# The dt product with its 32 weight columns as the stationary side, in four column groups

## The chip, the cores and the metric

The kernel runs on one core of a Trainium2 chip. The metric is the device time of one execution in microseconds (us). Each kernel is run several times and the median is taken. A profile is one further execution, recorded by the hardware profiler. Its span runs from the first to the last instruction, and all times in the rows below are counted from the span's start.

## The reference: what is computed

One layer of a hybrid trunk for 128 prompt tokens and 256 latent tokens, 384 in all. The normalised and modulated input `h` is multiplied by one wide matrix `w_in`, and the result feeds a Mamba-2 scan, an RWKV-7 scan, an output projection and a mixture of experts. The change touches the 32 columns of `w_in` that give `dt`, two directions of 16 heads each:

```
u = (h @ w_in).astype(jnp.float32)
...
z, xbc, dt_raw = jnp.split(u, [M_INNER, M_INNER + M_XBC], axis=-1)
xbc = jax.nn.silu(centred_depthwise_conv(xbc, conv_w, conv_b))
...
dt = jax.nn.softplus(dt_raw.reshape(bsz, seqlen, 2, M_HEADS) + dt_bias)
a = -jnp.exp(a_log.astype(jnp.float32))
...
la = jnp.moveaxis((dt * a_head).reshape(bsz, nc, M_CHUNK, M_GROUPS, e), 2, -1)
cs = jnp.cumsum(la, axis=-1)
```

So `dt_raw` is a product of 384 tokens by 1024 inputs by 32 columns. `dt` and `la` are then needed for the decays of the Mamba scan.

## The kernel before, in words

All is in float32. `hT` holds the input transposed, 8 tiles of 128 inputs by 384 tokens. The weights of `w_in` and of the conditioning matrix `w_ada` come in blocks of 512 columns (2 MB) through four slots (three in `ring_a`, one in `um_a`). The queue of SyncE (SP) issues the load of a block as soon as the block that had the slot before is used up, in one fixed order.

TensorE (PE) goes through a program written out by hand, in this order around the change:

- `project` (line 1655) with the 12 column tiles of x, B and C. ScalarE (ACT) copies each out, VectorE (DVE) sums the five taps of the convolution, ACT applies silu, PE transposes, DVE copies the token-major form (`token_major`, line 2329), from banks 4 and 5 of PSUM in turn.
- The Z loop (line 1697): six products of eight steps each, 128 tokens by 512 columns, ACT applies silu (line 2039).
- Between these stand the pieces of the conditioning product. `ada_block` (line 1613) has `cond` with 32 columns as the stationary side, in four column groups: each group takes two of the eight input tiles and writes 32 partitions of one bank. ACT copies the bank to `adas` (line 2009). `ada_columns` (line 1623) adds the four groups and transposes, by four products of a 128x128 tile of `adas` with `sel32`, a selector of ones.
- The dt product (line 1711), behind the Z loop and the last conditioning pieces: for each of three token tiles eight steps with a 128x128 tile of `hT` as the stationary side and 32 columns of `wdt` as the moving side, 24 products into bank 7.
- `project` with the 27 column tiles of the RWKV half (counted t = 0 to 26), into banks 0 and 1 in turn. After t = 1 PE does `decay_sums` (lines 1719 to 1724), which waits for `la`, and `scores` (line 1733); after t = 2 `states_in` (line 1745), which waits for the loaded SSM states; t = 0 to 2 use one weight block, t = 3 to 6 the next.

Behind the dt product DVE adds the bias (line 2340), ACT loads the table of exp and ln (line 2046) and takes exponentials and the logarithm of the softplus (to line 2050), and DVE forms `dt` and `la` (to line 2352), which frees `decay_sums`. In ACT's program this stands behind the six silus of Z and the last two copies to `adas`. The semaphore `dt_ps` counts dt products, `act_m` ACT's steps on dt, `conv_tm` DVE's token-major copies.

The stages further on (the Mamba scan between the RWKV projections, the RWKV rounds, the output projection, the experts) are started by semaphores and slots that earlier work frees.

Of the kernel before, what the change touches and what calls it, by code (L numbers as in the profile page):

```python
# [10 lines left out]
ACT = mybir.ActivationFunctionType  # L11
# [6 lines left out]
P = 128  # L18
D = 1024
KT = D // P  # L20
NTILE = 3
T = NTILE * P
# [81 lines left out]
def program(nc, a, out):  # L104
    ctx = ExitStack()
    with ctx:
# [16 lines left out]
        sel32 = sb("sel32", [P, 32])  # L123
# [53 lines left out]
        st1 = xdw  # L177
        xd = scratch[:, 2048:3072].rearrange("p (b d c) -> p b d c", b=2, d=2)
        wkv_ld = st_tiles[0:64, :].rearrange("p (d c) -> p d c", d=2)
        hT_flat = hT[:, :, :].rearrange("p k t -> p (k t)")  # L180
# [1417 lines left out]
        def _(pe):  # L1598
# [90 lines left out]
            ada_columns(6)  # L1689

            for i in range(6):
                n, j = Z_N[i // 3], i % 3
# [7 lines left out]
                if j == 0:  # L1700
                    ada_columns(7 if i == 0 else 9)
                if j == 2:
                    ada_block(8 if i == 2 else 10)
                    ada_block(9 if i == 2 else 11)
                    ada_columns(8 if i == 2 else 10)
            ada_columns(11)

            pe.wait_ge(s_wdt, 16)
            for j in range(NTILE):
                for k in range(KT):  # L1710
                    mm = pe.matmul(ps[:, 7, 32 * j:32 * j + 32], hT[:, k, P * j:P * j + P], wdt[:, k, :],  # L1711
                                   start=(k == 0), stop=(k == KT - 1))
            mm.then_inc(dt_ps, 1)

# [261 lines left out]
        def _(act):  # L1976
# [57 lines left out]
            ada_copy(7)  # L2034
            conv_silu(XBC - 1)
            for i in range(6):
                act.wait_ge(proj, XBC + i + 1)
# [10 lines left out]
            act.activation(dtmp[:, :, :], dtmp[:, :, :], ACT.Exp).then_inc(act_m, 1)  # L2048
            act.wait_ge(act_m, 1)
            act.activation(dtl[:, :, :], dtmp[:, :, :], ACT.Ln, bias=1.0).then_inc(act_m, 1)  # L2050
# [210 lines left out]
        def _(dve):  # L2261
# [69 lines left out]
            for t in range(XBC):  # L2331
                taps(t)
                if t >= 3:
# [4 lines left out]

            dve.wait_ge(dt_ps, 1)
            chain.do(dve.tensor_tensor(dt[:, :, :], ps[:, 7, 0:96].rearrange("p (j h) -> p j h", j=NTILE),  # L2340
                                   drow[:, 0:32].unsqueeze(1).to_broadcast([P, NTILE, 32]), ALU.add))
            dve.scalar_tensor_tensor(dtmp[:, :, :], dt[:, :, :], -1.0, dt[:, :, :], ALU.mult,
                                     ALU.min).then_inc(dt_in, 1)
            dve.wait_ge(act_m, 2)
            chain.do(dve.tensor_scalar(la[:, :, :], dtmp[:, :, :], 1.0, None, ALU.add))
# [416 lines left out]
```

## Time and profile before

| what | value |
|---|---|
| median of 3 runs | 1160.0 us (1158.66 to 1160.59) |
| the profiled execution | 1157.79 us |
| its span | 1156.0 us, 34174 instructions |
| PE busy | 1092.4 us (94%) |
| PE weight loads busy | 692.8 us (60%) |
| DVE busy | 600.0 us (52%) |
| ACT busy | 338.8 us (29%) |
| GpSimd (POOL) busy | 127.8 us (11%) |
| chain that ended last | PE 91%, DVE 4%, issue 2%, ACT 1%, DMA 1% |
| moved by DMA | 206.80 MB, mean 179 GB/s |

The busy times of engines overlap, so they don't add up to the span. The chain that ended last follows the end of the kernel back through what each step waited for, and says which engine's work sets the time. A product in float32 shows as two records of PE and two weight loads (PEld), so 24 products are 48 records. PEclk is the granted clock of TensorE as a share of 2.4 GHz: 1.00 is 2.4 GHz and 0.50 is 1.2 GHz.

### The profile page before, as it was taken

The page shows a single profiled execution, that of the slowest core. Times are in us where ns is not written, and L with a number is a line of the kernel's source. Part 1 is how long each engine was busy: PE and PEld are TensorE (multiplying, and loading weights), DVE is VectorE, ACT ScalarE, POOL GpSimd, SP SyncE. Part 2 cuts the span into 40 slices and gives each one's busy share as a digit, 9 for nine tenths or more (in the row PEclk, how much of TensorE's full clock was granted, in tenths as well). Part 3 has the DMA queues.
Part 4 walks back from the last instruction along what each step waited for, and adds up shares of the span by engine and source line. Part 5 has one row for each costly group of instructions (what it writes and reads, how often), then busy time and mean ns, then how long its engine had stood idle before and what let it go on. Part 6 is the DMA issues. An engine that isn't in the chain of part 4 may idle for free.

```text
span 1156.0 us, 34174 instructions
## 1 busy us (share of the span) xinstructions
PE 1092.4 (94%) x15326; PEld 692.8 (60%) x15326; DVE 600.0 (52%) x1346; ACT 338.8 (29%) x792; POOL 127.8 (11%) x185
## 2 busy tenths in 40 slices
PE   5999999999999899999999999988999999999995
PEld 2755447666665576666666666665675555555543
DVE  1455002678857576575766667532673343334346
ACT  2222111444443454454535445322330000000002
POOL 6000000122003031130303113000000000000002
PEclk9999997999999899999999998989999999999999
DMA  9844643564220302021110201134388999999984
GB/s 329 318 146 155 238 171 118 164 164 146 92 73 1 92 29 77 20 74 40 48 59 28 77 20 40 31 112 115 113 356 338 416 417 416 417 415 416 367 345 164
DMA packets 82336, 206.80 MB, mean 179 GB/s; under 512 B 12852, under 2 KB 21399, under 8 KB 77591
## 3 DMA queue, kind: packets, MB, share of 16 engines
q1 hardware_dynamic: 74816, 186.71, 43.7%
q10 hardware_dynamic: 6519, 14.90, 3.6%
q0 software_dynamic: 864, 3.15, 0.8%
q8 instruction: 113, 1.85, 0.6%
q14 instruction: 24, 0.20, 0.1%
HBM read 193.15 MB, written 11.58 MB: 177 GB/s over the span
## 4 chain that ended last, share of the span: by engine, by line
PE 91%; DVE 4%; issue 2%; ACT 1%; DMA 1%; SPq 0%; DVEq 0%; PEldq 0%; ACTq 0%
PE ps L1655 17%; PE ps L1240 10%; PE ps L1229 8%; PE ps L560 6%; PE ps L623 5%; PE ps L1260 5%; PE ps L1697 4%; PE ps L1878 3%; PE ps L542 2%; PE ps L1613 2%; PE ps L1779 2%; PE ps L474 2%; PE ps L592 1%; PE ps L455 1%; PE ps L699 1%
## 5 line engine op out<-in xcount | busy, mean ns | idle before, releaser
L1655 PE MATMUL ps<-hT,ring_a 128*128 128x384 f32 x624 | 210.9, 493 | 0.9 <-DVE um_a L2382 0.9
L1655 PEld LDWEIGHTS ps<-hT,ring_a 128*128 128x128 f32 x624 | 117.4, 192 | 80.3 <-issue 5.3
L1229 PE MATMUL ps<-scratch,misc 128*128 128x128 f32 x864 | 99.6, 275 | 1.5 <-DVE misc L2714 1.5
L1229 PEld LDWEIGHTS ps<-scratch,misc 128*128 128x128 f32 x864 | 97.9, 192 | 3.1 <-issue 3.1
L1299 ACT ACTIVATE um_a<-ps 128x256 f32<-128x256 f32 x17 | 6.5, 383 | 271.9 <-PE ps L1240 271.9
L560 PEld LDWEIGHTS ps<-ring_a 32*32 32x32 f32 x6144 | 62.1, 105 | 36.9 <-issue 23.6
L2382 DVE SCALAR_TENSOR_TENSOR um_a<-ps,mum,um_a 128x252 f32<-128x252 f32 (+1 forms) x162 | 57.2, 409 | 51.1 <-ACT um_a L2060 50.1
L560 PE MATMUL ps<-ring_a 32*32 32x32 f32 x6144 | 70.6, 195 | 7.7 <-issue 7.7
L1240 PE MATMUL ps<-ring_a,um_a 128*64 128x512 f32 x288 | 63.4, 593 | 1.6 <-DVE um_a L1281 1.5
L1240 PE MATMUL ps<-misc,um_a 128*64 128x512 f32 x128 | 56.3, 592 | 1.4 <-DVE um_a L1281 1.4
L623 PE MATMUL ps<-ring_a,mixm 128*128 128x512 f32 x96 | 54.3, 647 | 0.0
L1293 DVE COPY um_a<-ps 128x256 f32<-128x256 f32 x17 | 7.2, 424 | 90.5 <-PE ps L1249 90.5
L1281 DVE COPY um_a<-ps 128x1024 f32<-128x1024 f32 x17 | 20.8, 1226 | 53.7 <-issue 49.8
L1240 PEld LDWEIGHTS ps<-ring_a,um_a 128*64 128x64 f32 x288 | 21.0, 137 | 42.1 <-issue 42.1
L2060 ACT ACTIVATE um_a<-ps,mum 128x384 f32<-128x384 f32 x27 | 15.7, 580 | 103.1 <-PE ps L1655 103.1
L1524 POOL TENSOR_SCALAR_AFFINE_SELECT mixm<-mixm 128x512 f32<-128x512 f32 x24 | 17.8, 763 | 254.3 <-DMA mixm<-decay_sum_rows 254.3
L1004 DVE COPY_PREDICATED ring_a<-lvl,ps 128x128 f32<-128x128 int32 x96 | 26.6, 277 | 34.9 <-PE ps L560 34.9
L976 DVE TENSOR_TENSOR ring_a<-ps,tri 128x512 f32<-128x512 f32 x48 | 30.6, 679 | 15.4 <-PE ps L542 15.4
L1592 POOL DMA_INDIRECT um_a<-expert_rows,wdt x2 | 2.1, 1052 | 330.3 <-PE ps L1240 330.0
L822 ACT ACTIVATE ring_a<-ps 128x128 f32<-128x128 f32 x96 | 26.3, 276 | 41.5 <-PE ps L560 40.4
L1613 PE MATMUL ps<-ring_a,cond 128*32 128x512 f32 x144 | 22.5, 752 | 12.8 <-DMA ring_a<-in_w_ada 10.4
L2340 DVE TENSOR_TENSOR dt<-ps,drow 128x96 f32<-128x96 f32 x1 | 0.3, 257 | 66.1 <-PE ps L1711 66.1
(451 smaller groups left out, 2033.7 us busy)
## 6 DMA issues: line engine op xcount, KB each, us to landing
ring_a<-in_w_in SPq DMA_DIRECT2D x10, 2048.0 KB, 11.2
ring_a<-in_w_ada SPq DMA_DIRECT2D x9, 2048.0 KB, 12.1
ring_a<-in_moe_w_gate SPq DMA_DIRECT2D x18, 1024.0 KB, 9.9
ring_a<-in_moe_w_up SPq DMA_DIRECT2D x18, 1024.0 KB, 12.0
ring_a<-in_moe_w_down SPq DMA_DIRECT2D x18, 1024.0 KB, 12.1
ring_a<-in_w_out SPq DMA_DIRECT2D x59, 256.0 KB, 2.6
misc<-in_moe_w_gate SPq DMA_DIRECT2D x16, 512.0 KB, 9.4
misc<-in_moe_w_up SPq DMA_DIRECT2D x16, 512.0 KB, 12.1
```

The source lines that it names most:

```text
L560: mm = pe.matmul(ps[r, 2 * s + 1, m:m + 32], lhs[r, h, d, :], rhs[r, h, d, :], start=True, stop=True, tile_position=(32 * q, 32 * q), skip ...
L623: pe.matmul(ps[:, 7, :], src, mamba_w[n % RING], start=(k == 0), stop=(k == last)).then_inc(half_ps, 1)
L976: ins = dve.tensor_tensor(gk[p][:, h].rearrange("p d a t -> p (d a t)"), src, tri[:, :, :].rearrange("p i t -> p (i t)"), ALU.mult)
L1004: dve.copy_predicated(xc[s], level_mask(l, False), ps[:, 2 * s + 1, P:2 * P].rearrange("p (h d q) -> p h d q", h=2, d=2)).then_inc(x_ok, 1)
L1229: mm = pe.matmul(ps[:, k // 4, P * (k % 4):P * (k % 4) + P], h2[:, j, P * k:P * k + P], pick[:, j, :], start=(j == 0), stop=(j == NTILE - 1))
L1240: mm = pe.matmul(ps[h, 2 + b, :], xgT[:, b, k, h], gate_up_tile(b, x, k), start=(k == 0), stop=(k == KT - 1), tile_position=(0, CH * x), s ...
L1260: mm = pe.matmul(ps[h, 5 + c, :], hidT[:, b, k, h], wdn[b][x][:, k, BLK * c:BLK * c + BLK], start=(k == 0), stop=(k == 1), tile_position=( ...
L1613: mm = pe.matmul(ps[32 * q:32 * q + 32, ada_bank(i), :], cond[:, 2 * q + k2, :], slot(n)[:, 2 * q + k2, :], start=(k2 == 0), stop=(k2 == 1 ...
L1655: mm = pe.matmul(ps[:, t % 4 if isinstance(t, int) else t, 0:T], slot(n)[:, k, P * c:P * c + P], hT[:, k, :], start=(k == 0), stop=(k == K ...
L1697: mm = pe.matmul(ps[:, i % 4, :], hT[:, k, P * j:P * j + P], slot(n)[:, k, :], start=(k == 0), stop=(k == KT - 1))
L1878: mm = pe.matmul(ps[:, 2 * j + c, :], um_a[:, k, P * j:P * j + P], wout_tile(k)[:, BLK * c:BLK * c + BLK], start=(k == first), stop=(k == ...
L2382: ins = dve.scalar_tensor_tensor(dst, src, mum[:, m, t:t + 1], dst, ALU.mult, ALU.add)
```

## The change

The dt product is turned round. `dt_groups` takes the 32 columns of `wdt` as the stationary side, in four column groups like `ada_block`, and streams the 384 tokens of `hT` through: eight products, 32 partitions a group, in bank 4. ACT copies the bank to `dts`, a free row of `um_a`. `dt_tokens` adds the four groups and transposes to token-major by three products of a 128x128 tile of `dts` with `sel32`, into bank 5, from which DVE now reads. `dt_groups` stands ahead of the Z loop and waits for the token-major copy that read bank 4 last; `dt_tokens` stands behind the second Z product. The 24 products behind the last conditioning piece are gone.

```diff
+        dts = um_a[:, 17, :]
...
             ada_block(7)
             ada_columns(6)
 
+            def dt_groups():
+
+                pe.wait_ge(s_wdt, 16)
+                pe.wait_ge(conv_tm, 9)
+                for k2 in range(2):
+                    for q in range(4):
+                        mm = pe.matmul(ps[32 * q:32 * q + 32, 4, 0:T], wdt[:, 2 * q + k2, :], hT[:, 2 * q + k2, :],
+                                       start=(k2 == 0), stop=(k2 == 1), tile_position=(0, 32 * q), skip_group_check=True)
+                mm.then_inc(dt_ps, 1)
+
+            def dt_tokens():
+
+                pe.wait_ge(act_m, 1)
+                pe.wait_ge(conv_tm, 10)
+                for j in range(NTILE):
+                    mm = pe.matmul(ps[:, 5, 32 * j:32 * j + 32], dts[:, P * j:P * j + P], sel32[:, :], start=True, stop=True)
+                mm.then_inc(dt_ps, 1)
+
+            dt_groups()
             for i in range(6):
...
                 if j == 0:
                     ada_columns(7 if i == 0 else 9)
+                if i == 1:
+                    dt_tokens()
                 if j == 2:
...
             ada_columns(11)
 
-            pe.wait_ge(s_wdt, 16)
-            for j in range(NTILE):
-                for k in range(KT):
-                    mm = pe.matmul(ps[:, 7, 32 * j:32 * j + 32], hT[:, k, P * j:P * j + P], wdt[:, k, :],
-                                   start=(k == 0), stop=(k == KT - 1))
-            mm.then_inc(dt_ps, 1)
...
             conv_silu(XBC - 1)
+            act.wait_ge(dt_ps, 1)
+            act.activation(dts, ps[:, 4, 0:T], ACT.Copy).then_inc(act_m, 1)
             for i in range(6):
...
-            act.wait_ge(act_m, 1)
+            act.wait_ge(act_m, 2)
             act.activation(dtl[:, :, :], dtmp[:, :, :], ACT.Ln, bias=1.0).then_inc(act_m, 1)
...
-            dve.wait_ge(dt_ps, 1)
-            chain.do(dve.tensor_tensor(dt[:, :, :], ps[:, 7, 0:96].rearrange("p (j h) -> p j h", j=NTILE),
+            dve.wait_ge(dt_ps, 2)
+            chain.do(dve.tensor_tensor(dt[:, :, :], ps[:, 5, 0:96].rearrange("p (j h) -> p j h", j=NTILE),
...
-            dve.wait_ge(act_m, 2)
+            dve.wait_ge(act_m, 3)
```

How the orders move is seen at three places. A row is one instruction, or several alike, with its line, what it writes and reads, its shape and the semaphores it waits for. The first place is PE at the start of the Z loop; here is the kernel before, from the last conditioning block to the second Z product:

```order
L1613 MATMUL ps<-ring_a,cond 32x512 x7
L1623 MATMUL ps<-sel,scratch 128x2 [waits ada_copied]
L1623 MATMUL ps<-sel,scratch 128x2 x3
L1697 MATMUL ps<-um_a,hT 128x512 [waits projection_read,block_in_slot_3]
L1697 MATMUL ps<-um_a,hT 128x512 x7
L1623 MATMUL ps<-sel,scratch 128x2 [waits ada_copied]
L1623 MATMUL ps<-sel,scratch 128x2 x3
L1697 MATMUL ps<-um_a,hT 128x512 [waits projection_read]
L1697 MATMUL ps<-um_a,hT 128x512 x7
```

And here the same stretch after the change, where the lines have moved on (Z is line 1717, `ada_columns` 1624, `dt_groups` 1698, `dt_tokens` 1707):

```order
L1624 MATMUL ps<-sel,scratch 128x2 x3
L1698 MATMUL ps<-hT,wdt 32x384 [waits conv_token_major,wdt_loaded]
L1698 MATMUL ps<-hT,wdt 32x384 x7
L1717 MATMUL ps<-um_a,hT 128x512 [waits projection_read,block_in_slot_3]
L1717 MATMUL ps<-um_a,hT 128x512 x7
L1624 MATMUL ps<-sel,scratch 128x2 [waits ada_copied]
L1624 MATMUL ps<-sel,scratch 128x2 x3
L1717 MATMUL ps<-um_a,hT 128x512 [waits projection_read]
L1717 MATMUL ps<-um_a,hT 128x512 x7
L1707 MATMUL ps<-sel,um_a 128x32 [waits conv_token_major,act_mamba_steps]
L1707 MATMUL ps<-sel,um_a 128x32 x2
```

Eight products with a wait of their own have come ahead of the first Z product, and three behind the second.

The second place is PE behind the Z loop, in the kernel before, from the last conditioning block to the first RWKV projection:

```order
L1613 MATMUL ps<-ring_a,cond 32x512 x7
L1623 MATMUL ps<-sel,scratch 128x2 [waits ada_copied]
L1623 MATMUL ps<-sel,scratch 128x2 x3
L1623 MATMUL ps<-sel,scratch 128x2 [waits ada_copied]
L1623 MATMUL ps<-sel,scratch 128x2 x3
L1711 MATMUL ps<-wdt,hT 128x32 [waits wdt_loaded]
L1711 MATMUL ps<-wdt,hT 128x32 x23
L1655 MATMUL ps<-hT,ring_a 128x384 [waits h_ready,projection_read,block_in_slot_1]
```

After the change the projections follow the column products directly:

```order
L1614 MATMUL ps<-ring_a,cond 32x512 x7
L1624 MATMUL ps<-sel,scratch 128x2 [waits ada_copied]
L1624 MATMUL ps<-sel,scratch 128x2 x3
L1624 MATMUL ps<-sel,scratch 128x2 [waits ada_copied]
L1624 MATMUL ps<-sel,scratch 128x2 x3
L1656 MATMUL ps<-hT,ring_a 128x384 [waits h_ready,projection_read,block_in_slot_1]
```

The 24 products of line 1711 are gone from between them.

The third place is ACT around the Z loop after the change: silu of the last convolution tile (line 2041), the copies to `adas` (2025), the new copy (2053), the silus of Z (2057) and the softplus (2064 to 2068):

```order
L2041 ACTIVATE misc<-scratch,pv 128x256
L2053 ACTIVATE um_a<-ps 128x384 [waits dt_in_psum]
L2057 ACTIVATE misc<-ps 128x512 [waits projection_in_psum] x3
L2025 ACTIVATE scratch<-ps 128x512 [waits ada_columns_in_psum,ada_in_psum] x2
L2057 ACTIVATE misc<-ps 128x512 [waits projection_in_psum] x3
L2025 ACTIVATE scratch<-ps 128x512 [waits ada_columns_in_psum,ada_in_psum] x2
L2064 ACT_TABLE_LOAD [waits softplus_input_ready]
```

Only the copy is new. The softplus keeps its place behind the last copies to `adas`.

## Rows read from the trace of the kernel before

**Rows 1.** Chain that ended last, 112 to 212: start us, us, what.

```profile
113.51 1.90 PE ps L1613 x16
...
118.10 0.98 PE ps L1623 x8
119.08 6.97 PE ps L1697 x16
126.06 0.79 PE ps L1623 x8
126.84 13.84 PE ps L1697 x32
...
170.51 1.93 PE ps L1613 x16
172.44 1.88 PE ps L1623 x16
174.32 9.52 PE ps L1711 x48
183.84 12.87 PE ps L1655 x32
196.71 0.82 PE ps L1719 x8
...
199.22 1.54 PE ps L1733 x12
200.76 5.16 PE ps L1655 x16
205.92 1.75 PE ps L1745 x16
207.66 4.52 PE ps L1655 x14
```

**Rows 2.** Quarter-microsecond windows, PE alone: length, busy, PEclk, DMA share, GB/s.

```profile
174.75:175.00 0.25, 0.25 (x5) 1.00 0.97 336
175.00:175.25 0.25, 0.25 (x4) 0.56 0.98 377
...
188.50:188.75 0.25, 0.25 (x1) 0.63 0.00 0
188.75:189.00 0.25, 0.25 (x2) 1.00 0.00 0
```

**Rows 3.** Windows by stage: length, busy PE, PEld, DVE, ACT, POOL; PEclk, DMA.

```profile
113.30:119.00 5.70, 4.89 (x43) 1.89 (x41) 3.84 (x7) 2.60 (x8) 0.00 (x0) 1.00 0.83 286
...
140.70:154.00 13.30, 12.49 (x65) 5.80 (x66) 0.00 (x0) 2.39 (x4) 0.00 (x0) 1.00 0.95 342
...
225.00:342.00 117.00, 117.00 (x513) 77.57 (x513) 89.42 (x188) 55.70 (x154) 14.60 (x19) 1.00 0.37 117
```

**Rows 4.** Timeline of DVE: start us, us, what [idle before <-releaser].

```profile
116.77 1.01 DVE L2329 COPY misc<-ps 128x384 f32<-128x384 f32 x2
...
183.87 0.26 DVE L2340 TENSOR_TENSOR dt<-ps,drow 128x96 f32<-128x96 f32 x1 [66.09 <-PE ps L1711]
...
186.49 0.21 DVE L2345 TENSOR_SCALAR la<-dtmp 128x96 f32<-128x96 f32 x1 [2.07 <-ACT dtl L2050]
...
188.93 0.26 DVE L2352 SCALAR_TENSOR_TENSOR la<-dt,drow 128x96 f32<-128x96 f32 x1
```

**Rows 5.** Timeline of ACT.

```profile
118.65 0.79 ACT L2025 ACTIVATE misc<-scratch,pv 128x128 f32<-128x128 f32 x2
...
126.09 0.60 ACT L2039 ACTIVATE misc<-ps 128x512 f32<-128x512 f32 x1 [6.66 <-PE ps L1697]
...
172.50 0.60 ACT L2009 ACTIVATE scratch<-ps 128x512 f32<-128x512 f32 x1 [2.13 <-PE ps L1613]
...
184.45 1.28 ACT L2046 ACT_TABLE_LOAD   x1 [11.35 <-DVE dtmp L2342]
...
191.66 0.58 ACT L2060 ACTIVATE um_a<-ps,mum 128x384 f32<-128x384 f32 x1 [5.21 <-PE ps L1655]
```

**Rows 6.** DMA issues at 172.4 and 173.2: KB each, us to landing.

```profile
ring_a<-in_w_in SPq DMA_DIRECT2D x1, 2048.0 KB, 7.9
...
um_a<-in_state_ssm_fwd SPq DMA_DIRECT2D x1, 512.0 KB, 9.3
um_a<-in_state_ssm_bwd SPq DMA_DIRECT2D x1, 512.0 KB, 11.4
```

**Rows 7.** SP's queue at these issues: start us, us, what.

```profile
172.49 0.37 SPq L1359 DMA_DIRECT2D ring_a<-in_w_in  x1
172.90 0.58 SPq L1367 DMA_DIRECT2D um_a<-in_state_ssm_fwd  x1
173.53 3.17 SPq L1367 DMA_DIRECT2D um_a<-in_state_ssm_bwd  x1
```

**Rows 8.** Windows in the RWKV rounds, columns as in rows 3.

```profile
460.00:470.00 10.00, 9.04 (x256) 7.12 (x258) 6.44 (x13) 6.74 (x19) 6.50 (x7) 0.83 0.13 38
```

## Prediction

> **What bounds the kernel now.** I read the chain of work that ended last first, around the place of the change. From 113.5 to 212 it is TensorE nearly without a break: conditioning blocks (line 1613), column products (1623), Z (1697), the dt product (1711), the RWKV projections (1655) [rows 1]. The reader should see the 24 dt products there in person, 9.52 us from 174.32, with nothing ahead of them but PE's own work. Time taken from PE at this place is time taken from the kernel, as long as nothing else becomes late.
>
> Then I read the row behind it. Two projections take 12.87 us at 183.84, while the one at 200.76 takes 5.16 [rows 1]. Two should take 10.32, so 2.55 us are lost, and by work that the diff doesn't touch. The fine windows say why: the granted clock reads 1.00 until 175.0, falls to 0.50 (1.2 GHz) there, and is back at 1.00 only at about 188.7, 4.8 us after the dt product has ended [rows 2]. PE is busy in every one of these windows; it is the kind of work that differs: small products, each behind a full weight load. So the dt product runs mostly at half clock and leaves the half clock to the projections.
>
> Last I looked at who waits for it. DVE sits idle 66.09 us until the dt product ends, forms `la` by 189.19, and `decay_sums` starts at 196.71 [rows 1, 4]. So the softplus behind the dt product is hidden by two projections and sets nothing. From 225 to 342 PE is busy 117.00 of 117.00 us [rows 3], so what is won here is still won when the projections end.
>
> **What the change removes.** (a) The 24 products: 9.52 us. (b) The slow part of the projections, if the half clock goes with the products that came with it: 12.87 - 10.32 = 2.55 us. Together 12.07 us.
>
> **What it adds on PE.** (c) `dt_groups`: eight products with 32 stationary columns in four column groups. The nearest row is `ada_block`, the same eight products in the same four groups with 512 moving columns: 1.90 us [rows 1]. With 384 columns that is 1.90 x 384/512 = 1.43 us. Upper bound: were the groups not to overlap, the eight products would stream like one projection of the same 384 columns, 5.16 us. Lower bound: 1.43, since the columns must pass. I take 1.43, since the row differs only in the column count. (d) `dt_tokens`: three products 128x128 by 32 columns. Four products by 48 columns take 0.82 us [rows 1], 0.205 each; by 2 columns 0.79 for four, 0.20 each; six by 128 columns 1.54, 0.257 each. So three take 0.59 to 0.77 us; I take 0.62. Added: 2.05 us.
>
> **Waits that it adds.** `dt_groups` waits for the ninth token-major copy. The eighth and ninth of these (two copies together, counted from zero) run from 116.77 to 117.78 on DVE [rows 4], and PE is not there before 119.08 [rows 1]. It is hidden by the conditioning pieces with 1.3 us to spare; uncovered it would hold PE, and Z behind it. The new ACT copy, 0.58 us by the copy of the same size [rows 5], starts when `dt_groups` ends at about 120.5; ACT has ended its silu at 119.44 and sits idle until 126.09 [rows 5]. Queued behind it is only the first silu of Z, which then is not ready before 127.5. `dt_tokens` comes after two Z products, at about 135, 14 us after that copy. All three cost nothing. The softplus stays where ACT's program has it, behind the last copy to `adas`, which ends at 173.10 [rows 5], or 175.15 with the 2.05 us. Before, from the table load at 184.45 to `la` at 189.19 it was 4.74 us [rows 4, 5]; so `la` is there at about 179.9. `decay_sums` is reached at 176.37 + 10.32 = 186.7, so 6.8 us of cover are left.
>
> **Transfers behind it.** SP's program is the same. The next weight block and the two SSM states are issued at 172.49, 172.90 and 173.53 [rows 7], when the last conditioning block is used up, and land 7.9, 9.3 and 11.4 us later, the last at 184.9 [rows 6]. With the 2.05 us that is 187.0. `states_in` needs them at 205.92 [rows 1], now at 195.9; the block is needed for t = 3 at 207.66, now 197.6. About 9 us to spare. All later loads wait on PE's or others' progress and move along.
>
> **Sum.** 12.07 - 2.05 = 10.02 us. The profiled execution took 1157.79, so 1147.8 by its own account; it lies 2.2 below the median of the runs. What will be measured stands against the median: 1160.0 - 10.0 = 1150.0 us.
>
> One rule of the Trainium skill speaks against the change: its page "TensorEngine Tiling (Array Packing)", section "Tiling Modes", says that changing the tiling mode drains TensorE, and `dt_groups` puts 32-column tiles between two full-array products. The rows show the same switch already, from the conditioning block to the column products, and the latter start at 118.10 with no gap to what ended before [rows 1]. Were each of two more drains to cost one small product, 0.26 us, the gain would be 9.5 us by that rule; by the rows it stays 10.0.
>
> **Rivals.** B: the clock falls all the same. It fell 0.7 us after the dt product began, and ahead of that stood column products of 1.88 us [rows 1, 2], which stay and now lead straight into the projections. Then (b) is not won: gain 7.5, 1152.5 us. Against it: the like stretches at 113.3 and 140.7, with a pause and blocks and column products of 0.98 us, keep 1.00 [rows 3]. For it: two sets of column products in a row stand only here. [...]
>
> C: the four groups don't overlap, because the weight tiles of `wdt` or the single-bank output hold them in line. Then (c) is 5.16, gain 6.3, 1153.7 us. Against it: `ada_block` has the same form, bank and partitions included, and streams eight times 512 columns in 1.90 us.
>
> D: no change, because the dt product's time was cover for something that now comes late: the states or the block for t = 3. They would have to land 9 us later than reckoned to be felt at all and 19 us later to eat the whole gain: 1160 us. Nothing in the rows delays them; SP issues the same list.
>
> E, the other side: the clock falls ahead of Z instead of behind it, since `dt_groups` lengthens the stretch of small and narrow products from 113.5 to 119.1 by 1.43 us, and stays low in Z. Z's six products take 2 x (6.97 + 13.84) = 41.6 us [rows 1], the second weight block taking as long as the first, and double at half clock. Slower than before by 0.2% (2.3 us) begins where 12.3 us of them run doubled; all of them would give 1191 us. Against it: dense products brought the clock back 4.8 us after they began [rows 2], which would cost some 2.5 us and not 12.
>
> **How the numbers follow.** Forecast 0.70, B 0.15, C 0.07, D 0.04, E 0.02, and 0.02 for a larger gain than summed. The predicted time is the forecast's, 1150.0. Downwards the range allows for the 2.2 us by which the profiled execution was below the median, and for one place less of half clock in the RWKV rounds, where such places come and go (a row of 10 us at 0.83 [rows 8] is a third at half clock, about 1.7 us lost): 1146.5, rounded. Upwards it takes in B and C: 1154. What a measurement of this kernel can tell from no change is about 0.2%, 2.3 us. Faster: 0.70 + 0.15 + 0.07 + 0.02 = 0.94; same 0.04; slower 0.02.
>
> **What would show it.** Right: eight products of line 1698 in some 1.4 us ahead of Z, three of line 1707 in 0.6 us, PEclk 1.00 from 170 to 195, each of the first two projections in 5.2 us, `decay_sums` some 10 us earlier with no wait for `la`, and the distance kept from there to the end. Wrong: a stretch of 0.50 behind the column products (B), 5 us for line 1698 (C), a wait of line 1761 (`states_in`) or of t = 3 on a DMA (D), half clock in Z (E), or a distance of 10 us at 200 that is gone by 850, which none of these cases explains.

## The result, and the profile after

The changed kernel takes 1154.99 us (median of 10 runs, 1149.84 to 1161.4) beside 1163.1 us of the kernel before (10 runs, the three first ones and seven taken with the changed kernel, 1158.66 to 1166.52): a ratio of 0.9938, 95% interval 0.9915 to 0.9961. It is faster, as forecast, but the time lies 1.0 us above the range and 5.0 us above the predicted time. By ratio, 1150.0 to 1160.0 would have been 0.9914, just outside the interval. Here and below, means and ratios leave out executions over 1.5% above the fastest of the same kernel in the same measurement: 1171.92, 1176.44 and 2677.64 us of the kernel before (98 of 101 stay), 1163.5 with 50 empty instructions, and 379.18 and 740.41 us of two shortened kernels.

At its place the change did what was said. The chain of waits of the changed kernel (start us, us, what), from the last conditioning blocks ahead of Z to `states_in`, with a piece of the RWKV rounds at its end that is used further below:

```profile
116.84 0.98 PE ps L1624 x8
117.82 1.43 PE ps L1698 x16
119.25 7.06 PE ps L1717 x16
...
127.10 6.97 PE ps L1717 x16
134.07 0.59 PE ps L1707 x6
134.66 6.95 PE ps L1717 x16
...
173.37 1.88 PE ps L1624 x16
175.24 10.43 PE ps L1656 x32
185.67 0.82 PE ps L1735 x8
...
189.72 5.16 PE ps L1656 x16
194.88 1.75 PE ps L1761 x16
...
762.66 0.58 PE ps L593 x28
763.24 3.92 issue
767.16 0.43 PE ps L593 x3
```

Against [rows 1]: `dt_groups` (L1698) takes 1.43 us and `dt_tokens` (L1707) 0.59 where the 24 products took 9.52, and the two projections behind the conditioning take 10.43 us where they took 12.87. From the first projection to `decay_sums` it was 42.41 to 196.71, 154.30 us; it is 41.15 to 185.67, 144.52 us. That is 9.78 us gained, where the sum had 10.02. The 0.24 us between them are 0.11 in the projections and some 0.12 in Z: the Z products behind `dt_groups` and `dt_tokens` take 7.06 and 6.95 us, where they took 6.97 and 6.92 (half of 13.84), and `dt_tokens` gives back 0.03.

The windows of the changed kernel (columns as in [rows 3]) show the clock at 1.00 behind the conditioning, where [rows 2] showed the fall. The last line is all of the RWKV rounds:

```profile
113.30:119.00 5.70, 4.89 (x48) 1.88 (x40) 3.12 (x6) 1.88 (x4) 0.00 (x0) 1.00 0.95 353
170.00:185.00 15.00, 14.19 (x71) 8.23 (x64) 5.29 (x19) 3.74 (x7) 0.00 (x0) 1.00 0.75 222
185.00:200.00 15.00, 15.00 (x80) 10.84 (x79) 8.79 (x20) 4.50 (x8) 0.00 (x0) 1.00 0.29 80
225.00:340.00 115.00, 115.00 (x503) 75.73 (x502) 86.18 (x184) 53.33 (x146) 17.05 (x21) 1.00 0.41 117
...
369.00:788.00 419.00, 385.45 (x11734) 270.74 (x11734) 251.02 (x605) 186.02 (x451) 71.60 (x70) 0.95 0.17 52
```

The waits that the prediction costed at nothing are seen on the timelines of ACT and DVE of the changed kernel. ACT:

```profile
119.31 0.49 ACT L2053 ACTIVATE um_a<-ps 128x384 f32<-128x384 f32 x1 [1.14 <-PE ps L1698]
...
174.04 1.28 ACT L2064 ACT_TABLE_LOAD   x1
```

DVE:

```profile
134.70 0.26 DVE L2358 TENSOR_TENSOR dt<-ps,drow 128x96 f32<-128x96 f32 x1 [18.17 <-PE ps L1707]
...
176.08 0.21 DVE L2363 TENSOR_SCALAR la<-dtmp 128x96 f32<-128x96 f32 x1 [40.84 <-ACT dtl L2068]
...
178.53 0.26 DVE L2370 SCALAR_TENSOR_TENSOR la<-dt,drow 128x96 f32<-128x96 f32 x1
```

The copy is done at 119.80, 14 us before `dt_tokens`; `la` is there at 178.79 and `decay_sums` begins at 185.67, so 6.9 us of cover are left (forecast: 6.8). `states_in` (L1761) starts where the projection ahead of it ends, 189.72 + 5.16 = 194.88, so no wait has come in.

Yet the profiled execution of the changed kernel took 1158.65 us, more than the 1157.79 of the one before. The missing time lies in one stretch, the RWKV rounds. Landmarks from the chains of waits, in us (the RWKV rounds go from `compact_grams` to the output projection; the last three columns are lengths):

| execution | first projection | `decay_sums` | rounds begin | output projection | place of the change | rounds | rest |
|---|---|---|---|---|---|---|---|
| before | 42.41 | 196.71 | 379.95 | 786.9 | 154.3 | 406.9 | 369 |
| changed | 41.15 | 185.67 | 368.92 | 787.65 | 144.5 | 418.7 | 369 |

The changed kernel is 11 us ahead at `decay_sums`, 9.8 of them won at the place of the change and 1.3 by an earlier first projection. It is still 11 us ahead where the rounds begin, and leaves them level. The code of the rounds is the same in both, so the study asks two things: whether each step at the place of the change is as told, and what takes 12 us in rounds that nobody touched.

### The profile page after: what moved, and what is told of

The parts are those of the page before. It is cut to its first block, busy times and chain, and to the rows that moved or that the text cites. A ratio compares the mean times of both kernels' runs of the same rounds, so it can differ in the third digit from the quotient of the medians.

```text
span 1156.9 us, 34125 instructions
## 1 busy us (share of the span) xinstructions
PE 1083.3 (94%) x15300; PEld 684.4 (59%) x15300; DVE 600.4 (52%) x1346; ACT 339.8 (29%) x793; POOL 128.0 (11%) x185
## 4 chain that ended last, share of the span: by engine, by line
PE 89%; DVE 4%; issue 3%; DMA 2%; ACT 1%; SPq 0%; DVEq 0%; PEldq 0%; ACTq 0%
PE ps L1656 17%; PE ps L1241 10%; PE ps L1230 8%; PE ps L561 6%; PE ps L624 5%; PE ps L1261 5%; PE ps L1717 4%; PE ps L1894 3%; PE ps L543 2%; PE ps L1795 2%; PE ps L1614 2%; DMA ring_a<-in_w_ada 2%; PE ps L475 2%; PE ps L593 2%; PE ps L456 1%
## 5 line engine op out<-in xcount | busy, mean ns | idle before, releaser
L1656 PE MATMUL ps<-hT,ring_a 128*128 128x384 f32 x624 | 208.4, 489 | 0.9 <-DVE um_a L2400 0.9
L1241 PE MATMUL ps<-ring_a,um_a 128*64 128x512 f32 x288 | 63.4, 593 | 1.7 <-DVE um_a L1282 1.7
L1261 PE MATMUL ps<-ring_a,um_a 128*64 128x512 f32 x144 | 32.9, 598 | 0.7 <-DVE um_a L1294 0.7
## 6 DMA issues: line engine op xcount, KB each, us to landing
ring_a<-in_w_ada SPq DMA_DIRECT2D x9, 2048.0 KB, 12.5
```

The source lines that it names most:

```text
L1241: mm = pe.matmul(ps[h, 2 + b, :], xgT[:, b, k, h], gate_up_tile(b, x, k), start=(k == 0), stop=(k == KT - 1), tile_position=(0, CH * x), s ...
L1261: mm = pe.matmul(ps[h, 5 + c, :], hidT[:, b, k, h], wdn[b][x][:, k, BLK * c:BLK * c + BLK], start=(k == 0), stop=(k == 1), tile_position=( ...
L1656: mm = pe.matmul(ps[:, t % 4 if isinstance(t, int) else t, 0:T], slot(n)[:, k, P * c:P * c + P], hT[:, k, :], start=(k == 0), stop=(k == K ...
```

## The experiments

The gains below are differences of the mean times, with 95% intervals; each kernel was measured beside the kernel before on the same chip. The ratios in front of them are those on record and are not worked out from these means; the two differ by up to 3.4 us (0.9892 is 12.5 us of 1160, where the means differ by 9.2).

**The same kernel again, and the same code elsewhere in the program.** The theories: either the later code loses time because the change moved it to another place in TensorE's instruction stream, or single executions scatter. The second kernel shifts all code behind the transposes by 50 instructions that do nothing:

```diff
+            for _ in range(50):
+                pe.sem_inc(idle, 1)
             def ada_block(i):
```

> The changed kernel once more, as the measure for the others. Theory 1 (the dt part is right, and what is missing of the 10 us is lost in the RWKV rounds, where TensorE waits for its own instructions): PEclk 1.00 from 170 to 195, decay_sums 9.5 to 11 us earlier than before, the rest of the difference between 370 and 785; total 6 to 10 us below the kernel before. Rival (scatter of the runs alone): the rounds take the same on average as before, so total 10 us below, within 2.

> Changed kernel with 50 more empty instructions on TensorE, early, where it waits for the first loads; the changed kernel has 50 fewer than the one before, so all later TensorE instructions stand again where they stood in the code before. Theory 1: the idle time of TensorE put down to issue between 370 and 790 goes back from 26 us towards the 17 us of before, and the total is 2 to 4 us below the changed kernel, near 10 us below the kernel before. Rival: same as the changed kernel within 1.5 us.

The changed kernel again: 0.993 [0.990, 0.996], 6.6 ± 3.0 us. With 50 instructions: 0.9892 [0.9859, 0.9926], 9.2 ± 3.2 us. In both profiles the place of the change takes 144.52 us again; the rounds took 416.7 us without the instructions and 415.4 with them. The two intervals overlap; by the times nothing is told apart yet.

**The kernel before, with its code where the changed kernel has it.** 206 such instructions in three places (30, 125 and 51), the first of them ahead of all work of TensorE.

```diff
         def _(pe):
+            for _ in range(30):
+                pe.sem_inc(idle, 1)
...
+            for _ in range(125):
+                pe.sem_inc(idle, 1)
...
             ada_block(0)
+            for _ in range(51):
+                pe.sem_inc(idle, 1)
```

> Kernel before with 206 empty instructions on TensorE in its first waits, so that its later code stands, counted modulo 256 instructions, where that of the changed kernel stands. Theory 1: 2 to 4 us slower than the kernel before, with more issue time in the RWKV rounds. Rival: same as before within 1.5 us.

1.0112 [1.0074, 1.0151], 15.5 ± 3.2 us slower. Its chain of waits tells why the total says nothing of the rounds:

```profile
1.60 8.16 DMA ring_a<-in_w_ada
9.76 15.03 issue
24.79 3.54 PE ps L1618 x16
```

The first weights are there at 9.76 and TensorE does nothing until 24.79: the empty instructions themselves are waited for at the start. (In the two profiles before and after, the first product starts at 16.97 and 22.54, behind its weights.) So the total can't answer the question; the rounds in this profile can, and are read below.

**The 24 products of before, moved into Z.** They keep their form and only change their place, to where `dt_tokens` stands in the changed kernel (bank 5 instead of 7).

```diff
+                if i == 1:
+                    pe.wait_ge(s_wdt, 16)
+                    pe.wait_ge(conv_tm, 10)
+                    for jj in range(NTILE):
+                        for k in range(KT):
+                            mm = pe.matmul(ps[:, 5, 32 * jj:32 * jj + 32], hT[:, k, P * jj:P * jj + P], wdt[:, k, :], ...)
+                    mm.then_inc(dt_ps, 1)
...
-            pe.wait_ge(s_wdt, 16)
-            for j in range(NTILE):
-                for k in range(KT):
-                    mm = pe.matmul(ps[:, 7, 32 * j:32 * j + 32], ...)
```

> Kernel before with its 24 dt products as they were, only moved behind the second Z product and into bank 5. If the half clock came from their place behind blocks and column products: they take 24 x 0.20 = 4.8 us at 1.00 and leave the projections at 1.00, gain 9.5 - 4.8 + 2.5 = 7.2 us. If such small products lower the clock wherever they stand: 8 to 9.5 us again, half clock behind them in Z, gain 0 to 1 us.

0.9981 [0.9949, 1.0013], 2.2 ± 2.8 us. Its chain of waits, with the projections at the old place last:

```profile
130.75 5.28 PE ps L1707 x48
136.02 8.64 PE ps L1697 x16
...
178.30 10.43 PE ps L1655 x32
```

Its windows, the last two at the fall and the rise of the clock:

```profile
130.75:136.00 5.25, 5.25 (x49) 5.25 (x49) 0.00 (x0) 0.60 (x1) 0.00 (x0) 1.00 0.00 0
136.00:140.00 4.00, 4.00 (x7) 1.68 (x7) 0.52 (x2) 0.00 (x0) 0.00 (x0) 0.57 0.01 4
...
136.25:136.50 0.25, 0.25 (x2) 0.13 (x1) 0.22 (x2) 0.00 (x0) 0.00 (x0) 0.90 0.00 0
139.75:140.00 0.25, 0.25 (x2) 0.22 (x1) 0.00 (x0) 0.00 (x0) 0.00 (x0) 0.78 0.00 0
```

At full clock the products cost 5.28 us, not 9.52. But the clock falls behind them here too, at about 136.4, some 0.4 us after the last of them, and is back at about 139.9. The Z product in that stretch pays: 8.64 instead of 6.97 us. The projections at the old place run at full clock (10.43). So each of the two expectations was half right, the first on the products and the second on the clock behind them, and neither gain came out. The fall goes with this form of product: it came behind quite different neighbours, and is gone from the place that the products left. Locally the move should gain 12.07 - 5.28 - 1.67 = 5.1 us; between the landmarks it is 154.3 - 149.4 = 4.9, half of what the changed kernel gains.

The Trainium skill's page "TensorE: Matmul & The Clock Gate", section "Why this matters for your kernels", asks for no long idle gaps of TensorE between bursts, to avoid drops mid-kernel. Here PE is busy in all of the 5.25 us of the products and in all of the 4 us behind them: staying busy was not enough.

**The same, cut short behind the projections.** To see the place of the change without the rounds, four kernels end there: rounds, output projection and experts are left out, and of the outputs only the SSM states are written. The fourth is the changed kernel without its column groups: all eight products go to the same 32 columns, so nothing can overlap, and only 32 rows are copied and transposed.

```diff
-                for k2 in range(2):
-                    for q in range(4):
-                        mm = pe.matmul(ps[32 * q:32 * q + 32, 4, 0:T], wdt[:, 2 * q + k2, :], hT[:, 2 * q + k2, :], ...)
+                for k in range(KT):
+                    mm = pe.matmul(ps[0:32, 4, 0:T], wdt[:, k, :], hT[:, k, :], start=(k == 0), stop=(k == KT - 1))
```

> Kernel before, ended on every engine after the RWKV projections: the RWKV rounds, the output projection and the experts are left out, and only the SSM states are written. It is the measure for the next three. By the trace of before the projections end near 380, so some 380 to 388 us. Theory 1 (the scatter between executions comes from the rounds) expects runs within 2 us of each other, apart from the first loads; the rival (scatter of the whole chip or of the first loads) expects them as far apart as in the whole kernel, over 8 us.

> Changed kernel, ended at the same place (same parts left out). If the sum of the prediction holds at its place: 10.0 us below the cut kernel before, within 0.7. If the dt part itself gains less than summed (7 to 8 us, as the whole kernel showed): 7 to 8 us below.

> Kernel before with the 24 dt products moved behind the second Z product, ended at the same place (same parts left out). By the trace of the moved kernel (5.28 us for the products, and 8.64 instead of 6.97 for the Z product behind them at half clock) it gains 12.07 - 6.95 = 5.1 us; if the whole-kernel figure (2 to 4 us) is what the move is worth, 2 to 4 us.

> Changed kernel with all eight products of the first step in one column group, added in PSUM, instead of in four (the sum over groups is then over one group of 32 rows), ended at the same place (same parts left out). If the four groups overlap: the eight products take 5.2 us instead of 1.4, gain 6.3 us over the cut kernel before. If the groups bring nothing: the same as the cut changed kernel within 0.7 us.

| cut kernel | median us (range) | median under that of the cut kernel before | first projection to `decay_sums` |
|---|---|---|---|
| before | 379.38 (376.58 to 381.12) | | 154.3 |
| changed | 370.68 (368.14 to 372.96) | 8.7 | 144.5 |
| moved | 376.42 (373.03 to 379.18) | 3.0 | 151.0 |
| one column group | 372.27 (372.22 to 374.81) | 7.1 | 148.7 |

The chains of waits at the places in question, of the cut kernel before:

```profile
173.03 9.78 PE ps L1713 x48
182.81 12.60 PE ps L1657 x32
```

of the cut changed kernel:

```profile
118.64 1.43 PE ps L1700 x16
...
176.06 10.43 PE ps L1658 x32
```

of the moved one, where the clock fell within the products already (6.64 instead of 5.28) and the product behind them paid again:

```profile
133.53 6.64 PE ps L1709 x48
140.17 8.91 PE ps L1699 x16
```

and of the one with a single column group:

```profile
116.02 5.28 PE ps L1699 x16
121.30 7.06 PE ps L1717 x16
...
177.60 10.43 PE ps L1658 x32
```

One group takes 5.28 us, four take 1.43: the overlap of the groups is worth 3.85 us here. The 5.28 us are just what the 24 products of before take at full clock, so turning the product round saves no time of its own without the groups; what it saves then is the half clock (the Z product behind takes 7.06 us and the projections 10.43). The landmarks show both parts: 9.8 us gained with four groups, 5.6 with one.

The times say the same less sharply. By the means the changed kernel gains 8.7 ± 2.2 us, which holds the 10.0 of the first expectation as well as the 8 of the second; the landmarks, 154.3 and 144.5, decide for the sum. The single group is only 1.6 us behind the changed kernel by the medians, since four of its five executions, but only two of the changed kernel's, have a mean clock of 1.00: between these it is 372.3 against 368.5. The move gains 3.7 ± 2.3 us, and 3.3 by the landmarks: less than its first expectation, since the clock fell earlier in this execution. And executions of the cut kernel before lie 4.5 us apart, neither within 2 nor over 8: some of the scatter is there before the rounds (a standard deviation of 1.7 us, where the whole kernel has 4.0).

**Once more: the kernel before as a control, 50 and 100 instructions, and a shorter filler.** The last one halves the filler products that stand there to keep the clock up while the first weights load (`keep_warm` with 12 instead of 24) and adds 98 empty instructions.

> The kernel before once more, for a second profile of its RWKV rounds and as the measure of what equal kernels differ by. Theory 1 (code position): rounds of 405 to 410 us and some 17 us of issue time again. Rival (scatter alone): rounds anywhere from 405 to 420 us, as in the other profiles; the first profile of before was then a lucky one. Time within 1.5 us of the kernel before for both.

> Changed kernel with 50 empty instructions on TensorE, once more. Theory 1: 9 to 11 us below the kernel before again. Rival: 7 us below, as the changed kernel without them (7.2, plus or minus 2, over both measurements).

> Changed kernel with 100 empty instructions, so that its code stands 50 instructions behind that of before. Theory 1 gives another value than with 0 and with 50, by 2 us or more from one of them, since other work comes to stand at the borders of the code pieces. Rival: the same as the changed kernel within 1.5 us.

> Changed kernel with 12 instead of 24 filler products in the wait for the first loads, and 98 empty instructions, so that its later code stands as in the kernel before. In profiles where the clock fell in the first loads the filler took 6.8 to 7.1 us and the first projection began at 41 to 42; where it did not, 5.5 us and 39.3 to 39.7, when the load that it covers has landed. With half of it every start should be at 39.3 to 39.7: 1 to 2 us less on average than the changed kernel with 50 empty instructions. If fewer fillers let the clock fall later in the start, the same or slower.

The kernel before against itself: 1.0007 [0.9973, 1.0042], so equal kernels measure equal. 50 instructions: 0.9899 [0.9853, 0.9945], 12.5 ± 3.9 us. 100: 0.9875 [0.9829, 0.9922], 13.2 ± 4.5. Shorter filler: 0.9921 [0.9893, 0.9948], 9.1 ± 2.6; its first projection begins at 39.43, as expected, but the total doesn't show it.

What counts most are the profiles. The same program with 50 instructions took 404.6 us for its rounds, against 415.4 in its first profile: 11 us of difference in one stretch. Two things in the chain of waits and the windows make up nearly all of such differences. One is "issue", time in which nothing that the profile shows holds TensorE; its longer pieces are called pauses here. The other is time at half clock. The table has all twelve profiles of whole kernels; "shift" is the number of instructions by which the later code of TensorE stands behind its place in the kernel before.

| execution | shift | rounds, us | issue in them, us | at half clock in them, us (windows of 10 us) |
|---|---|---|---|---|
| before | 0 | 406.9 | 16.5 | 34 |
| before, again | 0 | 410.2 | 19.2 | 34 |
| moved | 1 | 414.3 | 19.8 | 45 |
| changed and 50 | 0 | 415.4 | 20.4 | 44 |
| changed and 50, again | 0 | 404.6 | 17.2 | 26 |
| shorter filler and 98 | 0 | 410.2 | 19.6 | 34 |
| changed | -50 | 418.7 | 25.8 | 44 |
| changed, again | -50 | 416.7 | 23.1 | 44 |
| changed, third | -50 | 413.1 | 21.4 | 37 |
| before and 206 | 206 | 412.7 | 20.1 | 41 |
| changed and 100 | 50 | 413.2 | 21.8 | 37 |
| changed and 100, again | 50 | 406.8 | 20.4 | 24 |

Take the issue time and half of the time at half clock off the rounds, and 371 to 374 us are left in all twelve, where the rounds themselves go from 404.6 to 418.7. So the 12 us that the first profile of the changed kernel lost in its rounds are about 9 us more of issue time and 5 us more lost to the clock, less 2 to 3 us that this count doesn't explain. The kernel before, again, is at the edge of what the first theory expected (410 and 17), and with the 50 instructions the issue time is back at 20.4 and 17.2. (Behind the rounds, the five profiles with 50, 98 or 100 empty instructions take 370.7 to 372.4 us, the other seven 369.0 to 369.3; why is open.)

The largest pause is the 3.92 us at 763.24 in the chain above. It stands behind 28 of 32 records of one group of small products (L593; L592 in the kernel before). In the second profile of the changed kernel it stands behind the same record (and in the third, with 3.65 us):

```profile
759.24 0.68 PE ps L593 x28
759.92 3.82 issue
```

and in the kernel before with 206 empty instructions, too:

```profile
780.49 0.58 PE ps L592 x28
781.07 3.92 issue
```

In the kernel before the pause stands behind the third record of that group and is shorter, first profile and second:

```profile
762.53 0.23 PE ps L592 x3
762.75 0.84 issue
...
761.08 0.23 PE ps L592 x3
761.30 1.66 issue
```

In the other four profiles with a shift of 0 or 1 it is behind the third record as well, 1.11 to 1.65 us long. With a shift of 50 it is earlier, in the group before:

```profile
755.38 0.58 PE ps L593 x27
755.96 0.97 issue
```

From the third record to the 28th are 25 records with 25 weight loads, 50 instructions, just the shift; and a shift of 206 is one of -50 and 256 more. So the pause stays at one place of the instruction stream, counted in steps of 256 instructions, while the products move through it. It is not the data that TensorE waits for there. This is the theory of the code's place, and the profile that could say nothing by its total bears it out. At this pause it costs the changed kernel 2 to 3 us more than the kernel before, in four profiles of four with that place. Summed over the rounds the issue time is 20.1 to 25.8 us at shifts of -50 and 206, 16.5 to 20.4 at 0 and 1, and 20.4 and 21.8 at 50, so the whole effect is less sure than the one pause.

The changed kernel's DMA queues from 755 to 770 (packets, MB, share) say what is late there:

```profile
q1 hardware_dynamic: 813, 3.14, 54.4%
q8 instruction: 3, 0.05, 1.2%
```

Instructions come as packets of 16 KB on a queue of their own, three in these 15 us, while 3 MB of weights of the output projection pass on the same engines. The packet beside the largest pause lands at 765.56, and TensorE goes on at 767.16, 1.6 us later; the packet before had landed at 759.37. This is no single case. In the twelve profiles of the table and the two of the rounds without the later part (below) there are 225 pauses of over 0.45 us in the rounds, and each of them ends 1.1 to 1.6 us after an instruction packet has landed, though the packets are 4.6 us apart on average. So TensorE waits for its code in these pauses, as far as a trace can show it; no run took the packets away. The Trainium skill's page "Runtime: NRT & Kernel Launch", section "Instruction fetch mechanics", says that the cost of crossing such a block of instructions is mostly hidden. By number the traces agree, with 13 to 20 such pauses to 92 or 93 packets in the whole rounds; what is not hidden is up to 3.92 us at once.

The clock in windows over the rounds, of the kernel before:

```profile
380.00:787.00 407.00, 382.04 (x11734) 268.17 (x11734) 250.77 (x605) 185.24 (x451) 71.64 (x70) 0.96 0.17 53
```

and of the kernel with 50 instructions, second measurement:

```profile
368.00:773.00 405.00, 380.07 (x11722) 266.23 (x11706) 250.51 (x605) 186.12 (x452) 71.31 (x70) 0.97 0.17 54
```

It is 0.96 and 0.97, and 0.95 in the changed kernel above: 34, 26 and 44 us at half clock.

**Without the later part, and with fewer small products.** Two kernels end behind the rounds (output projection and experts left out), and two more leave out half of the 32x32 products in the rounds as well.

```diff
-            for h in range(2):
+            for h in range(1):
                 for d in range(2):
```

> Kernel before, ended on every engine behind the RWKV rounds (the output projection and the experts are left out, and with them the outputs but the SSM states). Measure for the next: some 780 to 795 us, with the scatter of the whole kernel (7 us and more between the lowest and the highest), since that scatter comes from the start and the rounds.

> Changed kernel, ended at the same place (same parts left out). If the rounds take back part of the gain: 6 to 8 us below e13. If it is lost behind the rounds or not at all: 9 to 10.5 us below.

> As e13, and half of the 32x32 products of the rounds are left out too, so that TensorE has a quarter less code in them. If the rounds scatter because TensorE waits for its code: issue time in the rounds below 8 us, and runs within 4 us of each other. If not: issue time near 17 to 20 us and the scatter as in e13.

> Changed kernel with the same parts left out as in e15. If waiting for code takes back part of the gain, it does so no longer: 9 to 10.5 us below e15. If the rounds take it back for another reason: 6 to 8 us below.

By the means the change gains 9.9 ± 3.4 us behind the rounds (medians 785.53 and 773.11) and 10.6 ± 3.8 us with half of the small products left out. The two intervals hold both of the gains that were expected, so the times don't decide. The profile of the changed kernel does say something of the large pause. Ended behind the rounds, it has it behind the same record, but with 1.45 us instead of 3.65 to 3.92:

```profile
749.88 0.58 PE ps L593 x28
750.46 1.45 issue
```

and its queues from 743 to 758 have the instruction packets without the weights:

```profile
q8 instruction: 3, 0.05, 1.4%
```

So where the code stands sets the place of this pause, and the later part of the kernel, whose weights load just then, most of its length. This is also why no loss of the changed kernel's rounds shows here: what lengthens the pause was left out.

The issue time in the rounds fell from 18.0 and 17.2 us to 8.5 and 10.1 us with half of the small products left out, but the scatter did not: standard deviations of 3.0 and 2.5 us with all products, 3.6 and 2.9 with half, where runs within 4 us of each other were expected. Waiting for code costs time, but it is not what makes most of the difference between executions.

**The last pair, side by side.**

> The changed kernel once more. If its gain of about 7 us (instead of the 10 that its first part shows) comes from where its later code stands in the program, it again gains 5 to 8 us on the kernel before and stands 2 to 4 us above the version with 100 empty instructions in front. If the missing part is chance of single executions, it gains 8 to 12 us here and stands within 2 us of that version.

> The changed kernel with 100 empty instructions in front, once more. Code position: 10 to 14 us under the kernel before, as the 13.6 us (means) of its first runs. Chance: it falls back to the changed kernel's own gain, 7 to 10 us.

0.9895 [0.9855, 0.9935] and 0.9897 [0.9856, 0.9938]; means 0.9 ± 3.5 us apart. Here the changed kernel gains 11.4 ± 3.5 us as it is. The theory of the code's place predicted 2 to 4 us between the two; chance predicted under 2. The values go with chance, but the interval holds both.

**All executions together.** Each run also has its mean granted clock. Over the 28 runs of the changed kernel the time goes from 1146.04 us to 1161.4 us and the clock from 0.986 to 0.971, with a correlation of -0.88; 0.01 of clock goes with 8.2 us. For 88 runs of the kernel before (clock 0.962 to 0.983) it is -0.86 and 7.6 us. So the executions differ largely by how much of the span TensorE spent at half clock.

## Why the prediction was right and wrong, point by point

**(a) and (c), (d): right.** 1.43 us for `dt_groups` as taken, by scaling a row with the same column groups; 0.59 for `dt_tokens`, the lower bound, where 0.62 was taken. On the drain that the Trainium skill's page "TensorEngine Tiling (Array Packing)", section "Tiling Modes", names for a change of tiling mode: the first Z product behind `dt_groups` took 7.06 us instead of 6.97, so 0.09 us at most are seen there, not the 0.26 that was taken for it. The 9.78 us by the landmarks lie between the 9.5 of that case and the 10.02 of the sum.

**(b): right.** 10.43 us, 0.11 above the 10.32 of the sum, at a clock of 1.00. The moved products showed that the half clock goes where this form of product goes. The mean clock bears it out over many runs: it rose from 0.9721 to 0.9785 on average, by 0.0064, and 13.7 us at half clock less (175.0 to 188.7, [rows 2]) are 6.85 of 1156 us, 0.0059.

**Waits and transfers: right.** `la` 6.9 us before `decay_sums`, no wait of `states_in` (194.88 follows 189.72 + 5.16), PE unbroken to 340.

**Rivals.** B, the clock falling all the same, did not happen: 1.00 behind the column products. C did not: 1.43, and 5.28 when the overlap was taken away. D did not. E did not: Z's first product took 7.06 us, where half clock would have doubled it.

**What failed** is "How the numbers follow", not a term of the sum at the place of the change. First the base. Three runs of the kernel before lay within 1.9 us, 1158.66 to 1160.59, and their median 1160.0 was taken for its time. With the next seven it was 1163.1, and over 98 it goes from 1150.87 to 1172.88 with a mean of 1161.4. This is 3.1 of the 5.0 us; 1.4 of them are a base that was low, the others the luck of those ten. Second the upper bound. 1154 was drawn from rivals B and C alone and has nothing for the scatter of executions; the allowances for it, 2.2 us for the profiled execution and 1.7 us for "one place less of half clock", were made downwards only. Yet executions of one program differ by 11 us in the rounds alone and by 15 us in all. The prediction had the cause in its hands (a row at 0.83 in the rounds, "where such places come and go", [rows 8]) and sized it as one place and one way; the rounds have 24 to 45 us at half clock, and it goes both ways. Over all 28 runs the changed kernel's mean is 1153.5 us, so it is chance too that the ten of the result lie just outside the range and not just inside it.

The other 1.9 us are a gain of 8.1 us between the medians, where the sum had 10.0. Here "the distance kept from there to the end" is what gave way: it held to the start of the rounds in every profile (183.2 us from `decay_sums`), but taking out 50 instructions of TensorE moved all later code, and the pause at L593 came to 3.65 to 3.92 us, where it is 0.84 to 1.66 in the kernel before. The prediction had no term for this. That these 2 to 3 us are the missing 1.9 is likely but not shown: the intervals of the times are as wide as the effect.

The sign that "none of these cases explains", a distance of 10 us at 200 that is gone by 850, is just what the two first profiles showed. They compare an execution of the kernel before that is 5.3 us under its median of ten with one of the longest of the changed one; the rounds of an unchanged program differ by as much.

**The size of the gain.** The changed kernel gains 7.9 ± 1.7 us over its 28 runs against 98 of the kernel before; with 50 or 100 empty instructions it is 12.0 ± 1.8 us over 23 runs, or 11.4 ± 2.1 over all 24. The local gain of 9.8 us lies between. The 4.1 ± 2.2 us between the two groups agree with the longer pause at a shift of -50, but go beyond it, and the pairs that ran side by side differ by 2.5 ± 3.5 and 0.9 ± 3.5 us. So the sign of a cost of the code's place is shown in the chain of waits, while its size in the times is open. What sets the amount of half clock in one execution of the rounds is open too; no run here took it away. The version with 100 empty instructions is the shortest that was measured, 0.9875 and 0.9897, and was not told apart from the changed kernel when run beside it.

## What to carry to other kernels

A product with few output columns and many stationary loads costs more than its own time: price also the clock that it leaves to its neighbours, and turn it round (few columns stationary, the long side moving, several column groups at once) before trying to find it a better place. For the effect, measure between two landmarks of the chain of waits that enclose the change; for the total, take the base from ten or more runs and the width of a range from how far executions of one program differ, in both directions, not from how close three of them lie. And look through the later code for pauses that end behind an instruction packet: a change of the number of instructions moves them, here to a place where one took nearly 4 us and not 1 to 2.

## What the runs showed of the hardware that was not expected

- The clock fell to half while PE was busy in every window, behind 5.28 us of products of 32 columns with a full weight load each (0.90 in the window at 136.25 and 0.57 from 136 to 140 in the moved kernel), and dense products ran some 3.4 us at that level.
- One program's stretch of 32x32 products took 404.6 us in one execution and 415.4 in another; run times follow the mean granted clock with about 8 us for each 0.01.
- TensorE stands still in the rounds for 16 to 26 us in all, in pieces of up to 3.92 us. All 225 pauses of over 0.45 us end 1.1 to 1.6 us after an instruction packet of 16 KB landed. The place of a pause is fixed in the instruction stream, in steps of 256 instructions: with 50 instructions less ahead of it the same pause came 25 products with their weight loads later.
- Beside the load of 3 MB of weights that pause took 3.65 to 3.92 us, and 1.45 us where the load was left out.
- 206 instructions that do nothing made the program 15.5 us longer: TensorE reached its first product at 24.79 with the weights there at 9.76. With 100 placed behind the transposes alone that gap was 8.14 us, with the total time no longer.
